# A recurrent layer's gate products as three rounded ones, with GpSimd splitting their operands

## The reference

```python
def rglru_scan(xc, w_a, b_a, w_x, b_x, lam, reverse):
    xb = xc.reshape(b, s, 16, 128)
    r = sigmoid(einsum('bshc,hce->bshe', xb, w_a) + b_a).reshape(b, s, 2048)
    i = sigmoid(einsum('bshc,hce->bshe', xb, w_x) + b_x).reshape(b, s, 2048)
    log_a = -8.0 * r * softplus(-lam)
    a = exp(log_a)
    u = sqrt(-expm1(2.0 * log_a)) * (i * xb)
    return scan(h -> a * h + u, reverse)

def rglru_layer(x, ...):
    xr, gate = split(rms_norm(x, norm_g) @ w_in, 2)
    xc = conv_b + 4-tap depthwise convolution of xr
    y = rglru_scan(xc, forward weights) + rglru_scan(xc, backward weights, reverse=True)
    return x + (y * silu(gate)) @ w_out
```

## Time and profile before

| what | us |
|---|---|
| median of 3 runs | 2185.42 (2184.95 to 2186.5) |
| profiled execution | 2185.92 |
| its span | 2184.1 |
| TensorE busy | 2129.5 |
| VectorE busy | 1214.4 |
| ScalarE busy | 855.9 |
| GpSimd busy | 221.2 |

### The profile page before, as it was taken

How to read it: one execution, slowest core, us unless ns; L and a number is a source line. 1 busy time by engine, 2 the same in 40 slices (tenths; PEclk the granted TensorE clock), 3 DMA queues, 4 the chain that set the end, 5 groups by cost and what they waited for, 6 DMA issues and landing times.

```text
span 2184.1 us, 29571 instructions
## 1 busy us (share of the span) xinstructions
PE 2129.5 (97%) x12238; PEld 1523.5 (70%) x12238; DVE 1214.4 (56%) x1983; ACT 855.9 (39%) x1385; POOL 221.2 (10%) x301
## 2 busy tenths in 40 slices
PE   7999999999999999999999999999999899999998
PEld 6868757877777777899888888888867433333333
DVE  3532982439888767875523466345342555444554
ACT  4335461358886444673322552324442111111112
POOL 2000000013331022463000000000001000000000
PEclk9999999999999999999999999999999999999999
DMA  7122112423322444301222221333445899999995
GB/s 250 59 65 92 56 39 74 136 87 97 97 73 88 165 130 136 117 14 49 77 97 97 97 97 39 117 114 116 154 174 207 325 420 420 420 420 420 420 420 237
DMA packets 115703, 366.60 MB, mean 168 GB/s; under 512 B 7952, under 2 KB 36944, under 8 KB 90352
## 3 DMA queue, kind: packets, MB, share of 16 engines
q1 hardware_dynamic: 105888, 329.34, 40.2%
q0 software_dynamic: 9168, 29.00, 4.0%
q10 hardware_dynamic: 512, 6.34, 0.7%
HBM read 358.44 MB, written 10.54 MB: 169 GB/s over the span
## 4 chain that ended last, share of the span: by engine, by line
PE 89%; DVE 7%; ACT 2%; issue 1%; DMA 0%; POOL 0%; SPq 0%; DVEq 0%; ACTq 0%; POOLq 0%
PE bank L963 39%; PE bank L1174 13%; PE bank L1718 10%; PE bank L1735 5%; PE bank L1743 3%; PE bank L1291 2%; PE bank L1187 2%; PE bank L1218 2%; PE bank L1283 1%; DVE resid L3378 1%; PE bank L1120 1%; PE bank L1708 1%; PE bank L1111 1%; DVE w_lo L2456 1%; PE bank L1080 1%
## 5 line engine op out<-in xcount | busy, mean ns | idle before, releaser
L2456 DVE TENSOR_TENSOR w_lo<-raw,w_hi 128x2048 fp32r<-128x2048 f32 x117 | 268.7, 2296 | 445.0 <-ACT w_hi L1851 444.8
L1851 ACT ACTIVATE w_hi<-raw 128x2048 fp32r<-128x2048 f32 x117 | 223.9, 1913 | 394.7 <-PE bank L963 358.4
L3378 DVE TENSOR_TENSOR resid<-bank,resid 128x512 f32<-128x512 f32 x244 | 154.0, 684 | 175.5 <-PE bank L1743 175.5
L963 PE MATMUL bank<-hT_hi,w_hi 128*128 128x512 f32 x512 | 200.5, 392 | 2.5 <-DVE y_lo L3074 2.3
L963 PE MATMUL bank<-hT_hi,w_lo 128*128 128x512 f32 x512 | 199.6, 390 | 0.0
L963 PE MATMUL bank<-hT_lo,w_hi 128*128 128x512 f32 x512 | 199.5, 390 | 0.0
L1718 PE MATMUL bank<-piece,xT 128*64 128x512 f32 x792 | 186.0, 594 | 0.0
L1174 PE MATMUL bank<-hT_hi,w_hi 128*128 128x512 f32 x432 | 173.9, 402 | 0.9 <-DVE hT_lo L2520 0.9
L1174 PE MATMUL bank<-hT_hi,w_lo 128*128 128x512 f32 x432 | 168.2, 389 | 0.0
L1174 PE MATMUL bank<-hT_lo,w_hi 128*128 128x512 f32 x432 | 168.1, 389 | 0.0
L1718 PEld LDWEIGHTS bank<-piece,xT 128*64 128x64 f32 x792 | 58.3, 137 | 116.1 <-issue 116.1
(11 more groups left out here) (625 smaller groups left out, 4174.2 us busy)
## 6 DMA issues: line engine op xcount, KB each, us to landing
piece<-expert_w_gate SPq DMA_DIRECT2D x52, 1024.0 KB, 21.0
piece<-expert_w_down SPq DMA_DIRECT2D x49, 1024.0 KB, 21.5
piece<-expert_w_up SPq DMA_DIRECT2D x47, 1024.0 KB, 23.2
raw<-w_in SPq DMA_DIRECT2D x40, 1024.0 KB, 5.1
raw<-even_w_in SPq DMA_DIRECT2D x18, 1024.0 KB, 5.2
raw<-odd_w_in SPq DMA_DIRECT2D x16, 1024.0 KB, 5.6
raw<-expert_w_gate SPq DMA_DIRECT2D x12, 1024.0 KB, 18.2
raw<-expert_w_up SPq DMA_DIRECT2D x12, 1024.0 KB, 20.3
```

The source lines that it names most:

```text
L963: mm = pe.matmul(out, st, mv, start=first and x == 0, stop=last and x == 2)
L1851: act.activation(split_to(m)[0][:], raw[n % RAW][:], ACT.Copy).then_inc(sem("hi_done"), 1)
L2456: dve.tensor_tensor(split_to(m)[1][:], raw[split_of[m] % RAW][:], f32(split_to(m)[0][:]), ALU.subtract).then_inc(sem("lo_done"), 1)
L3378: dve.tensor_tensor(r, psum[bank][:], r, ALU.add).then_inc(sem(name), 1)
```

## The change

The gate products become three products of float32r parts each, 12 instead of 4 a block. The gate weights are split by GpSimd ahead of the layer: after its stage mark for the output product it loads each block's weights (two loads of 128 KB), copies them to float32r, subtracts, and stores both parts (512 KB a block) to a new DRAM tensor `gate_dram`, waiting for the store of the block before. In the recurrent layer it loads a block's parts from there with one transfer. The inputs are split block by block on GpSimd into `xc_hi` and `xc_lo`, two buffers, with the split of block blk+1 ahead of the multiplications of block blk. The buffers lie in room that is free at that time. PE waits for the split and for the loaded weights; before it waited for `evac_dve` and the loads. Of the semaphore table only reused counts change.

```diff
+        gate_load(0)
+        gate_load(1)
+        for blk in range(RB):
+            cut, w = gate_cut[blk % 2], gate_raw[blk % 2]
+            pool.wait_ge(sem(f"gates_in{blk % 2}"), 32 * (blk // 2 + 1))
+            pool.tensor_copy(cut[:, 0], w[:]).then_inc(sem("cut_hi"), 1)
+            pool.wait_ge(*after("cut_hi", blk + 1))
+            pool.tensor_tensor(cut[:, 1], w[:], f32(cut[:, 0]), ALU.subtract).then_inc(sem("cut_lo"), 1)
+            pool.wait_ge(*after("cut_lo", blk + 1))
+            if blk:
+                pool.wait_ge(*after("cut_saved", 16 * blk))
+            load(gate_dram[blk], cut[:], "cut_saved")
+            if blk + 2 < RB:
+                gate_load(blk + 2)
+
...
         def gate_weights(blk):
-            for g, w in enumerate(("gate_a_w", "gate_x_w")):
-                load(gate_w[blk % 2][:, g], io[w][0][:, blk].rearrange("d c e -> c d e"), f"gates_in{blk % 2}")
-
+            load(gate_w[blk % 2][:], gate_dram[blk], f"gates_in{blk % 2}")
+
+        def split_input(blk):
+
+            src = panels[pn["xr"][blk // 2]]
+            pool.wait_ge(sem("evac_dve"), src["at"] + blk % 2 + 1)
+            if blk >= 2:
+                pool.wait_ge(sem("gate_done"), 4 * blk - 4)
+            pool.tensor_copy(xc_hi[blk % 2][:], xc[:, blk % XC]).then_inc(sem("cut_hi"), 1)
+            pool.wait_ge(*after("cut_hi", RB + blk + 1))
+            pool.tensor_tensor(xc_lo[blk % 2][:], xc[:, blk % XC], f32(xc_hi[blk % 2][:]), ALU.subtract).then_inc(sem("cut_lo"), 1)
+
+        pool.wait_ge(*after("cut_saved", 16 * RB))
         gate_weights(0)
         gate_weights(1)
+        split_input(0)
         for blk in range(RB):
+            if blk + 1 < RB:
+                split_input(blk + 1)
             for it in (2 * blk, 2 * blk + 1):
...
         def gates(blk):
 
-            src = panels[pn["xr"][blk // 2]]
-            pe.wait_ge(sem("evac_dve"), src["at"] + blk % 2 + 1)
-            pe.wait_ge(sem(f"gates_in{blk % 2}"), 32 * (blk // 2 + 1))
+            w, hi, lo = gate_w[blk % 2], xc_hi[blk % 2], xc_lo[blk % 2]
+            pe.wait_ge(*after("cut_lo", RB + blk + 1))
+            pe.wait_ge(sem(f"gates_in{blk % 2}"), 16 * RB + 16 * (blk // 2 + 1))
             for d in range(2):
                 for g in range(2):
                     n = 4 * blk + 2 * d + g
                     if n >= 4:
                         pe.wait_ge(sem("gate_sig"), n - 3)
-                    pe.matmul(psum[n % 4][:], gate_w[blk % 2][:, g, d], xc[:, blk % XC], start=True, stop=True).then_inc(sem("gate_done"), 1)
+                    for x, (part, v) in enumerate(((0, hi), (1, hi), (0, lo))):
+                        mm = pe.matmul(psum[n % 4][:], w[:, part, g, d], v[:], start=x == 0, stop=x == 2)
+                    mm.then_inc(sem("gate_done"), 1)
```

More of the change, by code:

```diff
@@ L180, in build @@
         "e_in10": ("y_odd", KD),
-        "e_in11": ("qkT_done", 3 * NT),
-        "e_in12": ("qkT_act", 2 * NT),
+        "cut_hi": ("qkT_done", 3 * NT),
+        "cut_lo": ("qkT_act", 2 * NT),
+        "e_in11": ("qkT_done", 3 * NT + 2 * RB),
+        "e_in12": ("qkT_act", 2 * NT + 2 * RB),
         "e_in14": ("g_M32", 2 * HEADS),
@@ L187, in build @@
         "e_in22": ("first_in", 32),
-        "mem_in": ("gain_in", 32),
+        "cut_saved": ("gain_in", 32),
+        "mem_in": ("gain_in", 32 + 16 * RB),
         "qkT_dve": ("y_mix", KD),
@@ L282, in build @@
     hT_dram = nc.dram_tensor("hT_dram", [P, KD, SEQ], F32R, kind="Internal").ap()
+    gate_dram = nc.dram_tensor("gate_dram", [RB, P, 2, 2, 2, P], F32R, kind="Internal").ap()
     hn_dram = dram("hn_dram", [SEQ + 1, D])
@@ L411, in build @@
     xc = view("xc", 7, [P, XC, SEQ])
-    gate_w = [view(f"gate_w{b}", 7, [P, 2, 2, P], at=12288 + 2048 * b) for b in range(2)]
+    spare_at = free_at + 4096
+    gate_raw = [nc.alloc_sbuf_tensor_at(f"gate_raw{b}", [P, 2, 2, P], F32, offset=spare_at + 2048 * b) for b in range(2)]
+    gate_cut = [nc.alloc_sbuf_tensor_at(f"gate_cut{b}", [P, 2, 2, 2, P], F32R, offset=(free_at, spare_at + 4096)[b]) for b in range(2)]
+    gate_w = [view("gate_w0", 7, [P, 2, 2, 2, P], F32R, at=12288), nc.alloc_sbuf_tensor_at("gate_w1", [P, 2, 2, 2, P], F32R, offset=free_at)]
+    xc_hi = [nc.alloc_sbuf_tensor_at(f"xc_hi{b}", [P, SEQ], F32R, offset=spare_at + 4096 * b) for b in range(2)]
+    xc_lo = [nc.alloc_sbuf_tensor_at(f"xc_lo{b}", [P, SEQ], F32R, offset=spare_at + 4096 * b + 2048) for b in range(2)]
     rgate = view("rgate", 5, [P, RB, SEQ])
@@ L802, in _, with gate_load @@
         together(pool, 7)
+        def gate_load(blk):
+            for g, w in enumerate(("gate_a_w", "gate_x_w")):
+                load(gate_raw[blk % 2][:, g], io[w][0][:, blk].rearrange("d c e -> c d e"), f"gates_in{blk % 2}")
+        gate_load(0)
[12 more added lines that the diff above has]
+                gate_load(blk + 2)
         load(scan_mask[:], io["c_scan"], "late_in")
```

## The result

The changed kernel took 2193.16 us, the median of seven runs from 2190.47 to 2195.39; the kernel before, on the same chip, took 2184.95 us, seven runs from 2182.73 to 2186.5. The ratio is 1.0041, with a 95% interval of 1.0031 to 1.0052. The kernel became 8.2 us slower. The forecast was no change (2185.5 us). The median lies inside the range given (2176 to 2194) with 0.8 us to spare, two of the seven runs lie above it, and it is 0.9 us above the price of the rival "slower". So the range held, but the point forecast missed the loss.

A forecast was written before the change was run, and what follows sets the result against it. TensorE bounds the kernel, VectorE some 5 us behind in the gate steps. TensorE's 11.4 us saving is eaten by VectorE's waits, net -0.1 us: 2186.0 less 0.5 to the median, 2185.5 us; range 2176 to 2194, 8 in 10.

The forecast's parts named there:

- rival "slower": Gate steps: a copy holds VectorE as long as a subtraction and VectorE's list decides, 2192.3 us; chance 0.20, dense hits included.
- the sum: Whole kernel: 2185.9 + 0.1 = 2186.0, less 0.5 to the median, 2185.5 us; TensorE's 11.4 us saving eaten by VectorE's waits.
- GpSimd ahead of the layer: Weight splits during the output product: 4.5 to 4.9 us a block, 72 to 78 us for 16, hidden before the gates.
- The shared read: Gate steps: a reading GpSimd instruction costs a VectorE instruction with two SBUF inputs 0.97 us, the convolution taps nothing.
- The bound: Gate steps: VectorE replaces TensorE as the bound once the work added on VectorE exceeds 0.7 us.
- Start of VectorE's list: VectorE's weight split at 520.57 us moves forward by 2.1 us, to 518.4, with the gates of blocks 0 to 2.
- the hit in the norm: Norm ending the output product: GpSimd still reading there costs 0 to 1.9 us; 0 was taken.
- X: Work added on VectorE up to the second rp_lo: 12.6 us, from eight of ten splits at 1.45 plus 1.0 for multiplications.
- The gate: End of the second rp_lo, which TensorE waits for: its product starts at 662.7 instead of 661.47 us, 1.2 us late.
- 12.5 - X: Recurrent layer: general form of the net gain in us where VectorE's list decides; -0.1 us forecast.
- Price of a copy: Gate steps: a GpSimd copy that hits costs VectorE 0.48 us, between 0 and 0.97.
- rival "between": Gate steps: a hit costs the whole GpSimd instruction, 1.27 us subtraction, 0.6 copy: 2189.1 us; chance 0.05 past the border.

The follow-up runs named there:

- the first experiment: The kernel before with the input splits added on GpSimd where the change puts them, their parts read by nobody: 2193.75 us against 2184.27, ratio 1.0044.

## Where the prediction held and where it was wrong

What held:
- TensorE saves 0.72 us a block; 0.71 was in the sum, and nine tenths of it arrive once the splits are gone.
- GpSimd ahead of the layer. These are its instructions by line (count, busy us, mean ns, idle before and its releasers):

```profile
L825 POOL TENSOR_TENSOR gate_cut<-gate_raw,gate_cut 128x512 fp32r<-128x512 f32 x16 | 20.6, 1284 | 1.4
L823 POOL CAST gate_cut<-gate_raw 128x512 fp32r<-128x512 f32 x16 | 12.4, 778 | 1.7 <-DMA gate_raw<-gate_x_w 1.6
...
L776 POOL DMA_DIRECT2D gate_dram<-gate_cut x16 | 9.2, 576 | 21.1 <-DMA gate_dram<-gate_cut 18.1 <-POOL gate_cut L825 3.0
```

  A copy takes 0.60 to 0.63 us undisturbed (0.6 in the sum), a subtraction 1.28. What the sum lacked are 18.1 us of waits for the store before. So the residual's store starts at 438.27, 437.0 on the time axis of before, not at 421 to 430. The work that was named as its cover, up to the first gates, was enough.
- The shared read: about 1 us for each subtraction or multiplication, nothing on the taps.
- The bound: VectorE, with TensorE waiting at w_lo and rp_lo.

What was off, in the order of the sum:
- **Start of VectorE's list.** 518.4 was forecast; it is 521.80, or 520.55 on the time axis of before, 2.2 us late. Of that 0.8 us is the hit in the norm, for which I had taken 0 out of 0 to 1.9. The other 1.4 us come from the step before, in which the sum had no new hits: from the weight split at 492.96 to that at 521.80 VectorE works 28.8 us, 3.4 us more than before (28.88 less 3.45 of idle time), and that is more than the idle time left to it.
- **X, the count of hits: the step that failed.** The list runs from 521.80 to 669.01 + 2.29 = 671.30, 149.5 us. Less the 131.7 us of work of before, X is 17.8 us, where 12.6 was forecast (counted one by one it is 34.2 - 15.8 = 18.4; the rows overlap slightly).

```profile
521.80 2.28 DVE L2500 TENSOR_TENSOR w_lo<-raw,w_hi 128x2048 fp32r<-128x2048 f32 x1
...
669.01 2.29 DVE L2770 TENSOR_TENSOR rp_lo<-rgate,rp_hi 128x2048 fp32r<-128x2048 f32 x1
```

  I had let eight of ten splits hit, "as the multiplications do", and one of the four multiplications that so far had met the taps. Ten of ten did, and four of four: VectorE now stands at the recurrence and not at the taps when the multiplications of blocks 7 and 11 run. The ratio of eight in ten came from a list that still had 9.2 us of idle time; the sum itself used that idle time up, and kept the ratio. The counts are shown. For the idle time as their reason speak the other kernels: where VectorE keeps idle time, 16 of the 20 multiplications hit (before, and before with splits beside the convolution), and where it has none, all 20 (the change, and the two with input splits for blocks 0 and 1 only or beside the convolution). Why a list without gaps also meets every split is argued: next to two-input instructions it offers GpSimd only the taps and a few floors.
- **The gate.** The sum let TensorE wait for VectorE in one place, the second rp_lo. The first is another, with 4.95 us against 0.81. In the changed kernel the second still decides. Where only the first does, "12.5 - X" fails: without subtractions X is 8.7 and the start 1.0 us late, which would be 2.8 us gained, and none is. With input splits for blocks 0 and 1 only, where the second decides, it holds: 12.5 - 3.4 = 9.1, and the stretch is 8.7 us shorter.
- **Price of a copy.** 0.48 was taken, 0.39 measured. Here the error goes the other way and is small. With the measured price and all hits the sum would have been X = 10 x (0.97 + 0.39) + 3.9 = 17.5.
- **The sum again.** With 17.8 for X and 2.2 for the start, 12.5 - 17.8 - 2.2 = -7.5 us, 2192.9 us. Measured: 2193.2. In the trace TensorE starts the second output unit 8.6 us late (671.35 after, 661.53 before, less 1.25), and the next norm's turns 8.0 us late. The profiled executions differ by 9.5. Of the other 1.5 us, 1.25 lie ahead of the attention layer's output product and 0.3 behind the layer, where the instructions are the same; they are within the spread of the executions.

The rival "slower" gave 2192.3 us, with eight of ten splits hit and all four of the multiplications that had met the taps. It came near by two errors against each other: its copy cost 0.97 instead of 0.39, and two splits too few were hit. So that it came out nearest is luck in the price and right in the words under it, that dense lists are hit more often; they should have been in the forecast and not beside it. The rival "between", with the whole GpSimd instruction as the price, is refuted for instructions apart from one another: the subtraction of 1.29 us costs 0.97, the copy of 0.62 us 0.39. With whole instructions and all hits X would be 10 x 1.87 + 4 x 1.27 = 23.8 and the time 2198.9. The Trainium skill ("SBUF — State Buffer", Who interferes with whom) has it that the one that issues second is blocked until the first has finished. The traces agree on who meets whom (taps, with one SBUF input, 4.50 us beside splits and 4.54 alone), and, other than the prediction says, on how long: in the changed kernel VectorE's instruction goes on 0.12 to 0.15 us before GpSimd's row ends. The prediction compared the hold with the whole of GpSimd's instruction, of which 0.3 us had passed when VectorE's started. The experiments without the copy go beyond it: several instructions together can hold one.

## What to carry to other kernels

When a second engine stands 5 us behind the first, its idle time is the budget of every saving on the first, and anything laid on a resource that it shares is paid for with that. Count what meets what in the state after the change: here a chain without idle time met every neighbour, and a share of hits taken from a list with gaps was too low. Look at every place where the first engine waits for the second, not only at the end of the list: time taken off the list behind such a place came to nothing. Then look for the stretch in which the second engine doesn't use what is shared. The same 16 splits cost 9.5 us beside the recurrence and nothing measurable beside the convolution.

## What the runs showed of the hardware

- A VectorE instruction with two SBUF inputs that starts beside a reading GpSimd instruction went on 0.12 to 0.15 us before the end of that instruction's row in the changed kernel. It costs what is left of it: 0.9 to 1.1 us of a subtraction or multiplication of 1.27 to 1.29 us, 0.2 to 0.5 us of a copy.
- A VectorE instruction with one tensor input and a column of scalars (128x1024, L2545 at 416.47) took 1.86 us beside a GpSimd subtraction and 0.75 alone.
- GpSimd instructions that read SBUF and follow each other without a wait can hold a VectorE scan through all of them: 3.64 us for three in a row, 5.5 us for four with the issue of a load between. With a wait of GpSimd for its own result in between it is 1.15 us. The same is seen without subtractions, where a scan that meets a copy and two multiplications takes 2.95 us more (608.00). All of these are scans; a product beside the first of two multiplications without a wait (rows 4, 580.81) came through between them. Whether it takes a scan was not tried.
- Some holds are not explained by who started first. In the kernel changed for blocks 0 to 7 a scan starts at 554.95, 0.89 us ahead of two multiplications (555.84 to 558.40), and takes 4.54 us. In the first experiment an instruction of 0.69 us starts at 527.92, 0.38 us ahead of a copy, and takes 1.03 us.
- A GpSimd copy of 128x512 from float32 to float32r takes 0.60 to 0.63 us, less than half of a subtraction (1.28 to 1.30), and costs a VectorE instruction beside it 0.39 us in the mean.
- Issuing a transfer of 512 KB took GpSimd 0.58 us, one of 128 KB in short runs 0.72 us: the larger one, in long runs, was the cheaper to issue.
